# Where six late modulation pieces are loaded: dead memory outside the weight ring

## What is computed

```python
for l in range(DEPTH):                                  # DEPTH = 2
    mod = (silu(cvec) @ adaln_w[l] + adaln_b[l]).reshape(B, 6, D_MODEL)
    h = x * (1.0 + mod[1]) + mod[0]
    y, states = mixer(h, w_in, ..., w_out)              # GLA for l = 0, mLSTM for l = 1
    x = layernorm(ALPHA * x + mod[2] * y)
    h = x * (1.0 + mod[4]) + mod[3]
    x = layernorm(ALPHA * x + mod[5] * hier_moe(h, ...))
```

## Time and profile before

| | us |
|---|---|
| median of 3 runs | 1175.39 (1172.97 to 1178.36) |
| the profiled execution | 1172.82 |
| its span in the trace | 1171.1 |
| TensorE busy | 1078.5 (92%) |
| VectorE busy | 548.6 (47%) |
| ScalarE busy | 350.1 (30%) |
| GpSimd busy | 98.3 (8%) |
| moved by DMA | 328.08 MB, mean 280 GB/s |

### The profile page before, as it was taken

One profiled execution on the slowest core, in us unless ns is written; L12 is line 12 of the kernel. 1 busy time (PEld: TensorE's weight loads), 2 busy tenths in 40 slices (PEclk: granted clock), 3 DMA queues, 4 the chain that ended last, 5 costly groups with the idle time before them and its releaser, 6 DMA issues.

```text
span 1171.1 us, 14031 instructions
## 1 busy us (share of the span) xinstructions
PE 1078.5 (92%) x4666; PEld 484.9 (41%) x4696; DVE 548.6 (47%) x1244; ACT 350.1 (30%) x600; POOL 98.3 (8%) x169
## 2 busy tenths in 40 slices
PE   6999999999778999999978999999978999999995
PEld 3344534435443333333335556645543333333332
DVE  2373232327534655565574223222765455555555
ACT  1453221402331222222314334242253122222213
POOL 4000000003311000000022000000430000000000
PEclk9999999999779999999988999999989999999998
DMA  9993548455598999999844224113479899999963
GB/s 372 421 389 154 202 180 334 176 205 200 224 406 329 400 410 395 420 400 415 337 166 186 69 103 144 63 45 116 149 289 371 335 404 402 416 402 402 395 259 122
DMA packets 51305, 328.08 MB, mean 280 GB/s; under 512 B 6144, under 2 KB 8784, under 8 KB 14528
## 3 DMA queue, kind: packets, MB, share of 16 engines
q1 hardware_dynamic: 44672, 299.92, 64.3%
q0 software_dynamic: 4832, 20.68, 4.6%
q10 hardware_dynamic: 1760, 6.94, 1.5%
HBM read 320.64 MB, written 6.88 MB: 280 GB/s over the span
## 4 chain that ended last, share of the span: by engine, by line
PE 73%; DMA 13%; DVE 6%; ACT 4%; issue 2%; SPq 1%; DVEq 0%; POOL 0%; ACTq 0%; POOLq 0%
PE bank L742 34%; PE bank L1200 17%; DMA ring<-in_w_moe 9%; PE bank L1237 7%; PE bank L1217 7%; PE bank L766 2%; DMA region<-h_store,toki 2%; DMA ring<-in_w_out 1%; PE bank L1252 1%; PE bank L1226 1%; PE bank L1177 1%; DMA ring<-in_w_mod 1%; PE bank L1209 1%; PE bank L781 1%; DVE lstat L1876 1%
## 5 line engine op out<-in xcount | busy, mean ns | idle before, releaser
L1200 PE MATMUL bank<-ring,region 128*64 128x512 f32 x976 | 225.4, 596 | 11.4 <-DMA ring<-in_w_moe 8.4
L742 PE MATMUL bank<-ring,hT 128*128 128x512 f32 x336 | 148.1, 596 | 0.0
L1200 PEld LDWEIGHTS bank<-ring,region 128*64 128x64 f32 x976 | 71.5, 137 | 134.7 <-issue 133.5
L1237 PE MATMUL bank<-region 128*128 128x512 bf16 x510 | 115.0, 379 | 5.1 <-issue 4.7
L1217 PE MATMUL bank<-ring,region 128*64 128x512 f32 x512 | 116.7, 598 | 1.0 <-ACT region L1742 0.9
L1752 ACT ACTIVATE region<-region 128x512 bf16<-128x512 f32 x60 | 37.7, 630 | 200.6 <-DVE region L2329 200.6
L742 PEld LDWEIGHTS bank<-ring,hT 128*128 128x128 f32 x336 | 62.8, 190 | 77.9 <-issue 76.8
L742 PE MATMUL bank<-ring,region 128*128 128x512 f32 x192 | 85.4, 597 | 4.8 <-ACT region L1700 1.6
L1237 PEld LDWEIGHTS bank<-region 128*128 128x128 bf16 x540 | 50.4, 98 | 81.3 <-issue 22.7
L2329 DVE TENSOR_TENSOR region<-bank,region 128x512 f32<-128x512 f32 x60 | 41.3, 691 | 86.4 <-PE bank L1217 86.4
L742 PE MATMUL bank<-hT,ring 128*128 128x384 f32 x224 | 75.8, 490 | 1.5 <-DMA ring<-in_w_in 1.5
(11 more groups left out here) (340 smaller groups left out, 1286.6 us busy)
## 6 DMA issues: line engine op xcount, KB each, us to landing
ring<-in_w_moe SPq DMA_DIRECT2D x195, 1024.0 KB, 8.8
ring<-in_w_mod SPq DMA_DIRECT2D x48, 1024.0 KB, 10.5
ring<-in_w_in SPq DMA_DIRECT2D x21, 1024.0 KB, 7.1
ring<-in_w_out SPq DMA_DIRECT2D x4, 1024.0 KB, 7.6
ring<-in_w_out SPq DMA_DIRECT2D x8, 512.0 KB, 6.8
region<-gate_store POOLq DMA_DIRECT2D x4, 1024.0 KB, 6.3
region<-in_lnrows POOLq DMA_DIRECT2D x4, 1024.0 KB, 9.2
h_store<-region ACTq DMA_DIRECT2D x6, 512.0 KB, 3.0
```

What stands on the lines that cost most here:

```text
L742: ins = pe.matmul(out, lhsT, rhs, start=start, stop=stop, skip_group_check=True)
L1200: ins = pe.matmul(bank[6][u * CAP:(u + 1) * CAP, :], xs[:, k, u * CAP:(u + 1) * CAP], places[u][:, at:at + 2 * DE], start=k == 0, stop=k = ...
L1237: ins = pe.matmul(bank[2 * t + y][:, :], onehot[:, t * P:(t + 1) * P], part[:, c], start=False, stop=False, skip_group_check=True)
```

## The change

The six pieces leave `PIECES`, so behind `w_out` the first expert pair is next in the ring. Each gets a home in memory that is dead by then (`late_home`): four in `region`, one in `st0`, one in `st`. SP issues them behind the last `w_out` piece: four when the last head's keys are turned and three heads' outputs are through, the two in `st0` and `st` when `heads_done` is reached. TensorE multiplies them at the same places in its program, from the new homes, and waits at each for all six together. To have a semaphore free, two pairs of others are made one: `first_at` 1 and 2, and `wgt_in` with `wgate_in`. `mod_rows(1, 2)` of VectorE waits for the third group of token sums, since the pieces no longer add to `used`.

```diff
 PIECES += [("out", 0, q, j) for q in range(G_OUT) for j in range(3)]
-PIECES += [("mod", 1, i) for i in range(18, 24)]
 N_EARLY = len(PIECES)
...
+LATE_MODS = range(18, 24)
...
+        late_home = [region[:, a:a + PIECE] for a in (12928, 0, 0, 17024, 14976, 3072)]
+        late_home[1] = st0.rearrange("p a b -> p (a b)")[:, 0:PIECE]
+        late_home[2] = st.rearrange("p a b c -> p (a b c)")[:, 0:PIECE]
...
-            "dve_step", "act_step", "pool_step", "heads_done", "wgt_in", "wgate_in", "ml_consts")}
-        first_at = [sem(f"first_at{j}") for j in range(3)]
+            "dve_step", "act_step", "pool_step", "heads_done", "gate_weights", "ml_consts")}
+        late_at = sem("late_at")
+        first_at = [sem(f"first_at{j}") for j in range(2)]
...
             def load_first(j):
-                sp.dma_start(first_in[j], A["w_in"][j]).then_inc(first_at[j], 16)
+                sp.dma_start(first_in[j], A["w_in"][j]).then_inc(first_at[min(j, 1)], 16)
+
+            def load_late(i):
+                sp.dma_start(late_home[i - LATE_MODS[0]], A["w_mod"][MROUNDS * KD + i]).then_inc(late_at, 16)
...
+                    if (l, n, what[3]) == (0, G_OUT - 1, 2):
+                        sp.wait_ge(S["kt_ready"], 2 * H)
+                        sp.wait_ge(S["og_ready"], H - 1)
+                        for i in (18, 21, 22, 23):
+                            load_late(i)
+                        sp.wait_ge(S["heads_done"], 1)
+                        for i in (19, 20):
+                            load_late(i)
                     continue
...
                 if what[0:3] == ("in", 0, 0):
-                    pe.wait_ge(first_at[what[3]], 16)
+                    pe.wait_ge(first_at[1], 2 * 16)
...
                 r, k = divmod(i, KD)
-                j = AT["mod", l, i][1]
-                w = piece("mod", l, i).rearrange("p (c n) -> p c n", c=CT)
+                late = l == 1 and i in LATE_MODS
+                if late:
+                    pe.wait_ge(late_at, 16 * len(LATE_MODS))
+                w = (late_home[i - LATE_MODS[0]] if late else piece("mod", l, i)).rearrange("p (c n) -> p c n", c=CT)
...
-                ins.then_inc(used[j], 1)
+                if not late:
+                    ins.then_inc(used[AT["mod", l, i][1]], 1)
...
-                    pe.wait_ge(S["wgate_in"], 16)
+                    pe.wait_ge(S["gate_weights"], 16)
...
-                    pe.wait_ge(S["wgt_in"], 64)
+                    pe.wait_ge(S["gate_weights"], 16 + 64)
...
-                g, j = AT["mod", l, r * KD + KD - 1]
-                dve.wait_ge(used[j], g + 1)
+                if (l, r) == (1, MROUNDS - 1):
+                    dve.wait_ge(S["tok_ps"], len(ROW_GROUPS))
+                else:
+                    g, j = AT["mod", l, r * KD + KD - 1]
+                    dve.wait_ge(used[j], g + 1)
```

More of the change, by code:

```diff
@@ L621, in _ @@
             ready(pool.memset(onet[:, :], 1.0))
-            pool.dma_start(wgate, A["wgate"]).then_inc(S["wgate_in"], 16)
+            pool.dma_start(wgate, A["wgate"]).then_inc(S["gate_weights"], 16)
             own(pool.memset(alpha_i[:, :], 0.0))
@@ L703, in _ @@
                     for y in range(4):
-                        pool.dma_start(wgt[:, :, 32 * y:32 * y + H], A["wgt"][y]).then_inc(S["wgt_in"], 16)
+                        pool.dma_start(wgt[:, :, 32 * y:32 * y + H], A["wgt"][y]).then_inc(S["gate_weights"], 16)
                     own(pool.memset(causal[:, :, :, :], 1.0))
```

## The result

| | before | after |
|---|---|---|
| median, 10 runs each | 1174.38 us | 1165.19 us |
| span of the profiled execution | 1171.1 us | 1163.4 us |
| TensorE busy | 1078.5 us | 1077.5 us |
| moved by DMA | 328.08 MB | 328.08 MB |

The ratio is 0.9917, with a 95% interval of 0.9894 to 0.9941: 9.7 us less, between 6.9 and 12.4. The prediction said 9.9 us less and 1165.5 us. That the second number comes within 0.3 us is in part luck: it starts from 1175.39, the median of three runs, and the ten runs of the kernel before have 1174.38, so a smaller gain than forecast ends at the same time. TensorE does the same work and DMA moves the same bytes; what has changed is when they move.

A forecast was written before the change was run, and what follows sets the result against it. Layer 0's stretch was taken as bound by late expert weights colliding with the gather. Terms -9.9 + 0 + 0 = -9.9 us, from the shown runs' median 1175.39, gave 1165.5 us; range 1160.0 to 1172.5.

The forecast's parts named there:

- The bound of the stage: Layer 0, mixer's end to experts' start: bound by expert weights that load late and collide with the gather.
- Term -9.9: Layer 0, first gather issue to first adding step: 61.3 us becomes layer 1's 51.3; -9.9 us.
- rival 1: Layer 0's gather: broadcast rows late or transposes at low clock, each in part; 1166 to 1169.4 us; chance 0.10.
- rival 2: Layer 0's row blocks and first expert product: clock waits for real matmuls; gain 4.6 us, 1170.8 us; chance 0.04.
- rival 4: Layer 0's experts up to the loop: clock stays at 1.2 GHz; +17.3 us, 1192.7 us; chance 0.04.
- Term 0 for the broadcast: Six late loads beside POOL's broadcast of gate and norm rows: rows land in time; 0, bounds 0 and +2.3 us.
- Terms 0 for the small edits: Merged semaphores and the new wait of `mod_rows(1, 2)` on VectorE: each costs 0 us.
- The shift of what is behind: From layer 0's expert loop on: same code and loads, so all behind shifts as a whole with the -9.9 us.

The follow-up runs named there:

- the collision put back: The changed kernel, with SP holding the first expert pair's six loads until TensorE's first group of token sums, so they move beside the gather: 1174.62 us.
- TensorE kept busy: The changed kernel, with products of no use added on TensorE where it waits for token numbers and the gather, in both layers: 1167.30 us.
- the other way round: The kernel before, with four of the first expert pair's six loads held until the last gathered rows have landed: 1174.21 us.

## Why the prediction was right, point by point

**The bound of the stage** was read rightly, and the collision put back shows it: it took the whole gain. So is the reading of the queue shares, 85.6% for the ring before and 79.1% with the collision back. The trace of layer 1 as a picture of the changed layer 0 served well: the gathers landed after 5.6 us where layer 1 said 5.7. Only the landing of the expert pieces was put a little early: the last went out at 288.8 and landed 12.9 us later, at 301.7 and not before 300, still 9 us ahead of the gather.

**Term -9.9.** Over the two profiles of each kernel, from the gather's issue to the first adding step, it was 61.3 and 62.2 us before, 52.6 and 53.8 after: -8.5. All of it is in *gather*, 22.5 us before and 14.0 after; *start* is 39.2 on either side. So the term was over-sized by 1.4 us: 0.3 for a difference in *start* that isn't there, the rest for taking one value of layer 1 as a price. That value has a spread of its own: from gather to product layer 1 took 12.9 us in the profile read, the least of all nine profiles without filling, which go up to 13.7 and have a mean of 13.35. What was mis-sized above all is the clock. In layer 1 it rose 4 us into the transposes, and I gave 8.3 as the gain if it stayed low for all five blocks. It stayed low nearly to their end: in the profile after it rose at about 323.6, 8 us into transposes that follow each other closely (windows of the changed kernel):

```profile
322.00:323.00 1.00, 1.00 (x7) 0.93 (x5) 0.00 (x0) 0.58 (x2) 0.00 (x0) 0.50 1.06 430
323.00:324.00 1.00, 1.00 (x6) 0.61 (x4) 0.00 (x0) 0.74 (x2) 0.00 (x0) 0.63 1.02 434
```

The five blocks took 324.75 - 315.22 = 9.5 us, the number given for that bound, with the hole of 0.51 us in it; run again, they took 9.2, and the clock rose at about 321. With the clock held high (TensorE kept busy) *gather* is 12.7. That half of rival 1 thus came nearly true. The clock still rose while TensorE did transposes alone, ahead of the first expert product, so the row used against the Trainium skill's rule on transposes ("TensorE: Matmul & The Clock Gate", Part 4) held: rival 2's first product at half clock didn't come, nor did rival 4. Only with the collision back, where holes lie between the blocks, did the clock stay low into that product.

**Term 0 for the broadcast.** The sum had DMA drained at 265.0 and the rows landed 0.7 us ahead of the need. With the stage 1 us later, it drained at 264.8 and the rows landed 0.6 us ahead. It was the right size with a small margin, and the margin didn't shrink (1.0 us) when all six loads were issued beside the broadcast. The rate behind it, 412 GB/s, was if anything low (432 and 428 in the windows above). The Trainium skill ("DMA: Bandwidth & Descriptors", section Bandwidth) gives about 358 GB/s for a core whose neighbour streams too and 425 for one alone; the windows agree with the second.

**Terms 0 for the small edits** left no wait in the trace. `mod_rows` on VectorE is still behind `toki`, and TensorE's piece 18 waits for nothing.

**The shift of what is behind** held on the whole: the median moved by 9.7 us by the ratio, the stretch by 8.5, inside the interval. Where the other 1.2 us would come from, if they are real, is open. The two profiles alone would have misled: their difference up to the first adding step was 375.52 - 363.51 = 12.0 us, in which 4.5 us of routing are the clock's spread, and of which 2.9 seemed to be given back in the loop, which the repeated profiles show to be spread as well (212.9 us in the kernel before, run again).

**What I argued too lightly**, in the expectation of the other way round, is that the weights only had to be out of the gather's way. The kernel with four of them behind it refutes that. No row of the trace before shows this wait, since there all six pieces had landed by the time TensorE came to them.

## What to carry to other kernels

When a small scattered transfer on the critical path is slow, look at which queue holds the DMA engines' time beside it; if it is prefetch, move the prefetch into a stretch where DMA idles, and not merely to the other side of the small transfer, where the same bytes came back here as 11 us of waits in the next 32 us. Dead memory outside the ring is a way to do that, since a ring lets nothing be loaded ahead of what it holds. And if the same code runs elsewhere in the kernel without the suspected neighbour, its rows are a good price, once their own spread is known.

## What the runs showed of the hardware that I had not expected

The granted clock over the same instructions differed from one execution to the next: in the stretch from 291 to 304 us it was 1.2 GHz for 13 us or for 3 us in the kernel before, and for 3 us or not at all in the changed one. Between 13 us and none lie 6 us of 1170. That is two thirds of this change's gain, and it makes a single pair of profiles a poor measure of it. The other is how mildly the broadcast took the ring beside it: its second half landed in 14.2 us beside 6.3 MB and in 7.2 us without them, where the six gathers beside the same queue went from 5.6 to 14.9 us (median).
